# First attention of a two-layer block: last query rotation among the taps, ten taps moved, modulation products one tile later, row copy ahead of the exponentials

## The chip, the cores and the metric

The kernel runs on one core of one Trainium2 chip. The metric is the device time of one execution in microseconds (us). TensorE, VectorE, ScalarE and GpSimd are called PE, DVE, ACT and POOL, as the profile calls them. SP only issues transfers.

## The reference

Two transformer layers run on 1024 tokens of width 1024, all in float32. The change lies in the first layer. There the projection gives queries, keys and values of 8 heads of 64 and the two halves of a gated convolution. Queries and keys are rotated by position. Each token (a 16 x 64 grid) attends to a window of 8 x 16 neighbours and to 256 context tokens. Beside it a depthwise convolution of 31 taps runs over the gated half.

```python
def rope_half(xh, pos):                      # x1*cos - x2*sin, x2*cos + x1*sin
...
s_win = einsum(q_rot, k_window) * scale + bias      # 8 x 16 neighbours, biased by offset
s_ctx = einsum(q, k_ctx) * scale                    # 256 context keys, not rotated
p = softmax(concatenate([s_win, s_ctx]))
out = p_win @ v_window + p_ctx @ v_ctx
conv_x = silu(layer_norm(depthwise_conv(a * sigmoid(b), 31 taps) + bias))
x_new = x + g1 * (concatenate([attn, conv_x]) @ w_out)      # g1, sh2, sc2, g2: columns of silu(c) @ w_ada
```

The last line's g1 and the second norm's scale and shift are the "modulation": a product of one vector with a 1024 x 6144 matrix, of which 4096 columns (32 rows of 128) are computed during the attention, since they are not needed sooner.

## The kernel before, in words

Each engine runs its own instruction list in order, and the lists meet by semaphores. `sem(...)` names a counter, `reach(e, name, n)` makes engine e wait for it, and `free[0]` and `free[1]` count when the two halves of the accumulator `region` may be written again. `ch(...)` issues a DVE instruction and waits for it before the next one.

The projections come in units of 128 output columns. The last ones are u (gated half), k, v and q, four query units of two heads each. After a query unit ACT copies it twice (L748, L750). DVE rotates the second copy in `proj1_dve`: a shuffle (L797), two products (L798, L799) and two adds (L801). POOL splits the weights of later units into a high and a low part (L3006, L3009).

The attention (`na_*`) has 32 tiles. A tile is two heads and 128 queries (8 x 16 of the grid) against 640 keys. Tile i passes the engines so:

- PE, `scores(i)`: one row of the late modulation (`late_pe`, L630, into spare columns of `region` half 0), the turn of the row before (`late_turn_pe`, L636), then the scores (L971 context, L975 window).
- DVE, `most(i, s)` for the two heads s: adds the bias, writes `na_prob` and keeps the extreme (L1089). ACT, `exps(i, s)`: exponential with its sum (L1048). `late_act(i)` copies the modulation row out (L296, `late_row`). In before it runs between the two exponentials and gives `region` half 0 free.
- `norm(i)` one tile later: DVE takes the reciprocal (L1098) and scales one head (L1101), ACT the other (L1054). PE, `turn(i)`, transposes by matmul (L987, L992) in its own round i + 2. ACT moves four blocks of each head back to SBUF (`move`, L296, `na_prob_t`), DVE the fifth of both (L1107).
- PE, `values(i)`, in round i + 3: probabilities times values (L1008). ACT and DVE store the result as a high and a low part (`hi`, L296 `mixa_hi`; `lo`, L1113).

Beside this DVE works off the 124 convolution taps (`conv_tap`, L1164, 128x1024, in place on `conv`): 80 in the projection, 44 in the attention, one or two per tile. POOL adds finished groups of `conv` (`conv_sum_pool`, L1174). These three sums wait for all rotations and for 62, 93 and 124 taps.

SP's queue holds, in order, the loads of biases (384 KB, four buffers), of values (`v_pair`, 4 transfers of 64 KB a call) and of modulation weights (512 KB, two buffers, `late_load`). A late load waits until the row two before it is multiplied.

Of the kernel before, what the change touches and what calls it, by code (L numbers as in the profile page):

```python
# [25 lines left out]
ALU = mybir.AluOpType  # L26
ACT = mybir.ActivationFunctionType
# [3 lines left out]
T = 1024  # L31
# [4 lines left out]
CTX = 256  # L36
# [5 lines left out]
HD = 64  # L42
# [63 lines left out]
def build(nc, x_t, ctx_t, mem_t, w_ada, w_ada_late, units, small, rope_c, rope_s, na_bias, positions, out, x_spill,  # L106
# [58 lines left out]
    cos1 = place("cos1", [T], 160)  # L165
    late_row = place("late_row", [P], 178)
    v_ctx_raw = fixed("v_ctx_raw", [2, CTX], 28 * KIB)

# [469 lines left out]
    def late_act(e, n):  # L638
        reach(e, "late_used", 4 * (n + 1))
        copy(e, late_row[:], late_out).then_inc(sem("late_row"), 1)  # L640
        reach(e, "late_row", n + 1)
        e.sem_inc(free[0], 1)

# [61 lines left out]
    def proj1_act(e, pos, ch):  # L705
# [34 lines left out]
        for j in range(4):  # L740
            use = pos.next_use()
            e.wait_ge(unit_done, UNIT0["q"] + j + 1)
            if j < 2:
                reach(e, "v_tr", 3 + j)
            else:
                reach(e, "rope_done", 3 + j)
# [3 lines left out]
            e.activation(tmp[:, 2 + j % 2], region[:, use % 2], ACT.Copy, scale=HD ** -0.5).then_inc(free[use % 2], 1)  # L750
            if j == 0:
                v_out_act(3)

    def proj1_dve(e, pos, ch):
# [31 lines left out]
        for j in range(4):  # L786
# [3 lines left out]
            some_taps(6)  # L790
        for j in range(4):
            if j == 1:
                v_ctx_dve(e, 3)
            use = pos.next_use()
            e.wait_ge(free[use % 2], use // 2 + 1)
# [4 lines left out]
            for rb in range(2):  # L800
# [3 lines left out]
                else:  # L804
                    ch(last)
            reach(e, "rope_done", 5 + j)
        return taps

# [144 lines left out]
    def na_pe(e, pos):  # L953
        assert pos.use % 2 == 0

        def scores(i):
            j, q = divmod(i, TT)
# [6 lines left out]
            rows = [slice(0, 64), slice(64, 128)]  # L964
            for s in range(2):
                wait_region(e, uses[s])
            late_pe(e, i)
            if i:
                late_turn_pe(e, i - 1)
            for s in range(2):  # L970
# [44 lines left out]
        for i in range(NA_N + 3):  # L1015
# [4 lines left out]
            if i == NA_N:  # L1020
                wait_region(e, pos.use + 1)
                late_turn_pe(e, N_LATE - 1).then_inc(sem("late_tr"), 1)
            if i == NA_N + 1:
                wait_region(e, pos.use)
                ln_mean_pe(e)
# [4 lines left out]
    def na_act(e, pos, ch):  # L1030
# [25 lines left out]
        for i in range(NA_N + 4):  # L1056
            if i >= 4:
                hi(i - 4)
            if 1 <= i < NA_N + 1:
                norm(i - 1)  # L1060
            for s in range(2):
                if i < NA_N:
                    exps(i, s)
                if s == 0 and i < NA_N:
                    late_act(e, i)
                if 2 <= i < NA_N + 2:
                    move(i - 2, s)
# [8 lines left out]
    def bias_of(i):  # L1076
        j, q = divmod(i, TT)
        return 6 * j + 3 * (q // 4) + [0, 1, 1, 2][q % 4]

    def na_dve(e, pos, ch, taps):  # L1080
        def most(i, s):
# [5 lines left out]
            if s == 0:  # L1087
                reach(e, f"bias_ld{n % 4}", 16 * (n // 4 + 1))
            e.tensor_tensor_reduce(na_prob[:, i % 3, s], region[:, s, 0:KEYS], bias_t[n % 4][:, s], -1.0, 3.0e38,  # L1089
                                   ALU.add, ALU.min, na_neg[:, c:c + 1]).then_inc(sem("na_most"), 1)  # L1090
            if s:
                reach(e, "na_most", 2 * i + s + 1)
                e.sem_inc(free[s], 1)

# [15 lines left out]
        def lo(i):  # L1110
# [3 lines left out]
                            na_out(mixa_hi, j, q).bitcast(F32), ALU.subtract).then_inc(sem("na_lo"), 1)  # L1114

        left = list(taps)
        for n in range(1, 4):
            e.memset(bias_t[n][:, :, 0:CTX], 0.0).then_inc(sem("bias_zero"), 1)
        for i in range(NA_N + 4):
# [7 lines left out]
            if 2 <= i < NA_N + 2:  # L1127
                move(i - 2)
            for n in left[len(left) * i // NA_N:len(left) * (i + 1) // NA_N]:
                conv_tap(e, ch, n)  # L1130
            if i == NA_N:
                late_end_dve(e, ch)
                e.sem_inc(free[1], 1)
            if i > NA_N:
# [1778 lines left out]
    with nc.Block() as block:  # L2913
        @block.sync
        def _(sp):
# [30 lines left out]
            for cs in range(4):  # L2946
                v_pair_load(sp, 0, cs)
            late_load(0)
            late_load(1)
            reach(sp, "bias_zero", 4)  # L2950
            for n in range(1, 4):
                bias_load(sp, n)
            loads = iter(range(4, N_BIAS))
            for i in range(NA_N):
                if i + 2 < N_LATE:
                    late_load(i + 2)
# [405 lines left out]
```

## Time and profile before

| | us |
|---|---|
| median of three runs | 2526.86 (2525.43 to 2527.62) |
| the profiled execution's own time | 2529.12 |
| its span in the profile | 2527.3 |
| PE busy | 2407.3 (95%) |
| DVE, POOL, ACT busy | 1345.9, 968.6, 936.5 |
| mean granted clock of PE | 0.986 |

PE is busy for 95% of the span, but not evenly. The attention lies at 307 to 499 us, between the last query unit and the first output unit. There PE's share is lower (230 matmul records and 17.4 us busy in the 20 us from 420 to 440), and that stretch alone is changed.

### The profile page before, as it was taken

What the parts mean: (1) busy time and instruction counts of PE and PEld (TensorE: products, weight loads), DVE (VectorE), ACT (ScalarE), POOL (GpSimd) and SP (SyncE); (2) the same over time, 40 slices, a digit from 0 to 9 for tenths busy, and PEclk for the clock granted to TensorE, in tenths of its full rate; (3) what the DMA queues carried; (4) which work ended last, traced back from release to release, by engine and by line L of the source; (5) the groups of instructions that cost most, each with busy time, mean ns of one, the idle gap of its engine ahead of it and who ended that gap; (6) DMA issues with size and microseconds to landing.
All of it is one profiled execution on the core that took longest, in us unless ns stands there. A gap on an engine that the chain in (4) does not pass through costs nothing.

```text
span 2527.3 us, 34014 instructions
## 1 busy us (share of the span) xinstructions
PE 2407.3 (95%) x13374; PEld 1965.2 (78%) x13374; DVE 1345.9 (53%) x1566; ACT 936.5 (37%) x1541; POOL 968.6 (38%) x574
## 2 busy tenths in 40 slices
PE   6999888899999999999999899998999999999999
PEld 3788767677878888888877578877888888888877
DVE  3799678767732223222584977854410246454342
ACT  4301267625343234422554477752410111323220
POOL 1444300032255444544433310026134444787643
PEclk9999989999999999999999899999999999999999
DMA  6111266321121111111122300002011111111132
GB/s 268 42 42 57 83 186 184 114 88 45 43 63 51 42 55 62 56 34 55 54 109 67 143 25 2 1 26 84 18 50 50 42 50 51 66 52 43 50 125 92
DMA packets 66080, 175.12 MB, mean 69 GB/s; under 512 B 6724, under 2 KB 25416, under 8 KB 64392
## 3 DMA queue, kind: packets, MB, share of 16 engines
q1 hardware_dynamic: 59936, 149.66, 18.1%
q10 hardware_dynamic: 5992, 23.34, 2.4%
q8 instruction: 107, 1.75, 0.3%
q14 instruction: 45, 0.37, 0.0%
HBM read 161.89 MB, written 11.08 MB: 68 GB/s over the span
## 4 chain that ended last, share of the span: by engine, by line
PE 83%; DVE 10%; ACT 3%; issue 2%; DMA 1%; POOL 1%; SPq 0%; ACTq 0%; DVEq 0%; POOLq 0%
PE region L300 15%; PE region L302 15%; PE region L301 15%; PE region L2545 3%; PE region L2547 3%; PE region L2546 3%; PE aux L2545 3%; PE aux L2547 3%; PE aux L2546 3%; PE pv L2109 2%; PE aux L2099 2%; PE pv L300 2%; PE pv L301 2%; PE pv L302 2%; DVE conv L1164 1%
## 5 line engine op out<-in xcount | busy, mean ns | idle before, releaser
L3006 POOL TENSOR_TENSOR w_hi<-w_raw,der 128x1024 fp32r<-128x1024 f32 x96 | 192.3, 2003 | 889.8 <-PE region L302 834.8
L300 PE MATMUL region<-h_hi,w_hi 128*128 128x512 f32 x928 | 367.2, 396 | 10.6 <-issue 5.0
L301 PE MATMUL region<-h_lo,w_hi 128*128 128x512 f32 x928 | 364.4, 393 | 0.0
L302 PE MATMUL region<-h_hi,w_lo 128*128 128x512 f32 x928 | 363.7, 392 | 0.0
L2582 POOL TENSOR_TENSOR w_lo<-w_raw,w_hi 128x512 fp32r<-128x512 f32 x153 | 199.4, 1311 | 241.6 <-ACT w_hi L296 239.7
L3009 POOL TENSOR_TENSOR w_lo<-w_raw,w_hi 128x1024 fp32r<-128x1024 f32 x96 | 261.2, 2721 | 7.5
L300 PEld LDWEIGHTS region<-h_hi,w_hi 128*128 128x128 f32 x928 | 176.0, 190 | 54.9 <-issue 8.8
L302 PEld LDWEIGHTS region<-h_hi,w_lo 128*128 128x128 f32 x928 | 176.1, 190 | 37.3
L301 PEld LDWEIGHTS region<-h_lo,w_hi 128*128 128x128 f32 x928 | 176.1, 190 | 35.7
L296 ACT ACTIVATE w_hi<-w_raw 128x512 fp32r<-128x512 f32 (+1 forms) x159 | 100.2, 642 | 256.9 <-PE pv L302 85.1
L1164 DVE SCALAR_TENSOR_TENSOR conv<-glu,par,conv 128x1024 f32<-128x1024 f32 x120 | 188.2, 1568 | 3.4
L2582 POOL TENSOR_TENSOR w_lo<-w_slot,w_hi 128x512 fp32r<-128x512 f32 x57 | 75.3, 1327 | 107.6 <-ACT w_hi L296 107.1
L1438 DVE TENSOR_TENSOR ff_lo<-mlp_blk,ff_hi 128x512 fp32r<-128x512 f32 x56 | 50.1, 894 | 93.4 <-ACT ff_hi L296 93.3
L296 ACT ACTIVATE prob_t<-aux 128x512 f32<-128x512 f32 (+1 forms) x160 | 81.9, 554 | 47.6 <-PE aux L2099 37.3
L1609 DVE SCALAR_TENSOR_TENSOR x<-pv,der,x 128x1024 f32<-128x1024 f32 x28 | 35.9, 1283 | 117.8 <-PE pv L302 117.8
L2170 DVE TENSOR_REDUCE der<-region 128x1 f32<-128x1024 f32 x64 | 78.2, 1223 | 23.1 <-PE region L302 21.5
L300 PE MATMUL pv<-ff_hi,w_hi 128*128 128x512 f32 x224 | 87.8, 392 | 1.5 <-POOL w_lo L2582 0.8
L301 PE MATMUL pv<-ff_lo,w_hi 128*128 128x512 f32 x224 | 87.2, 389 | 0.0
L302 PE MATMUL pv<-ff_hi,w_lo 128*128 128x512 f32 x224 | 87.2, 389 | 0.0
L2545 PE MATMUL region<-h_hi,w_hi 128*128 128x512 f32 x204 | 79.4, 389 | 0.0
L2546 PE MATMUL region<-h_lo,w_hi 128*128 128x512 f32 x204 | 79.4, 389 | 0.0
L2547 PE MATMUL region<-h_hi,w_lo 128*128 128x512 f32 x204 | 79.4, 389 | 0.0
(481 smaller groups left out, 5884.8 us busy)
## 6 DMA issues: line engine op xcount, KB each, us to landing
w_raw<-units SPq DMA_DIRECT2D x122, 512.0 KB, 3.5
w_raw<-units SPq DMA_DIRECT2D x77, 256.0 KB, 2.6
w_raw<-w_ada_late SPq DMA_DIRECT2D x32, 512.0 KB, 4.3
bias<-na_bias SPq DMA_DIRECT2D x24, 384.0 KB, 4.0
w_slot<-units SPq DMA_DIRECT2D x35, 256.0 KB, 2.6
ada_buf<-w_ada SPq DMA_DIRECT2D x4, 2048.0 KB, 28.8
head_wide<-v_spill SPq DMA_DIRECT2D x16, 512.0 KB, 3.7
x_sb<-x_t ACTq DMA_DIRECT2D x2, 2048.0 KB, 14.1
```

The source lines that it names most:

```text
L296: return e.activation(dst, src, ACT.Copy, **kw)
L300: pe.matmul(dst, wh, xh, start=first, stop=False)
L301: pe.matmul(dst, wh, xl, start=False, stop=False)
L302: return pe.matmul(dst, wl, xh, start=False, stop=last)
L1164: ch(e.scalar_tensor_tensor(out=conv[:, j], in0=src, scalar=w, in1=conv[:, j], op0=ALU.mult, op1=ALU.add))
L2170: e.tensor_reduce(neg_max[:, m % 4:m % 4 + 1], region[:, s], AX, ALU.max, negate=True).then_inc(sem("mla_maxed"), 1)
L2545: e.matmul(dst, wh[:, w], xh[:, k], start=(j < 3 and k == 0), stop=False, skip_group_check=True)
L2546: e.matmul(dst, wh[:, w], xl[:, k], start=False, stop=False, skip_group_check=True)
L2547: last = e.matmul(dst, wl[:, w], xh[:, k], start=False, stop=(k == 3), skip_group_check=True)
L2582: e.tensor_tensor(w_lo[chunk_of(c)], chunks[c].src, w_hi[chunk_of(c)].bitcast(F32), ALU.subtract).then_inc(chunk_ready, 1)
L3006: pool.tensor_tensor(w_hi[:, s], w_raw[:, s], one_col.broadcast_to([P, 1024]), ALU.mult)\
L3009: pool.tensor_tensor(w_lo[:, s], w_raw[:, s], w_hi[:, s].bitcast(F32), ALU.subtract)\
```

## The change

Five things move, and no arithmetic is dropped.

1. The rotation of the fourth query unit leaves `proj1_dve`. It gets two buffers of its own (`q3_raw`, `q3_swapped`) and runs as four steps in DVE's rounds 2 to 5 of the attention. The unit is needed from tile 24 on.
2. Ten of the 44 taps left go into the query units (1, 3, 3 and 3), together with the three memsets of the bias buffers. 34 taps and the four rotation steps are spread over rounds 0 to 30, so none is left in round 31.
3. PE multiplies modulation row i - 1 in round i, behind the turn of row i - 2. The scores no longer wait for ACT's row copy but for DVE's `most` alone (`na_most`).
4. ACT copies row i - 1 after `most(i, 0)` and ahead of `exps(i, 0)`, and `hi` goes ahead of the second `move` instead of behind it.
5. SP's queue: bias 1 goes ahead of late load 1, the second pair's values move to rounds 5 to 8 behind the last rotation, and each round's late load goes last.

```diff
@@ late_act
         copy(e, late_row[:], late_out).then_inc(sem("late_row"), 1)
-        reach(e, "late_row", n + 1)
-        e.sem_inc(free[0], 1)
@@ proj1_dve
-        for j in range(4):
+        some_taps(1)
+        for j in range(3):
             if j == 1:
                 v_ctx_dve(e, 3)
+                some_taps(3)
+            if j == 2:
+                some_taps(3)
...
+        for n in range(1, 4):
+            e.memset(bias_t[n][:, :, 0:CTX], 0.0).then_inc(sem("bias_zero"), 1)
+        some_taps(3)
@@ na_pe
+        def late(n):
+            if n:
+                late_turn_pe(e, n - 1)
+            late_pe(e, n)
...
-            for s in range(2):
-                wait_region(e, uses[s])
-            late_pe(e, i)
             if i:
-                late_turn_pe(e, i - 1)
+                reach(e, "na_most", 2 * i)
+                late(i - 1)
+            else:
+                for s in range(2):
+                    wait_region(e, uses[s])
@@ na_act
-            if i >= 4:
-                hi(i - 4)
             if 1 <= i < NA_N + 1:
                 norm(i - 1)
             for s in range(2):
+                if s == 0 and 1 <= i < NA_N + 1:
+                    reach(e, "na_most", min(2 * i + 1, 2 * NA_N))
+                    late_act(e, i - 1)
                 if i < NA_N:
                     exps(i, s)
-                if s == 0 and i < NA_N:
-                    late_act(e, i)
+                if s == 1 and 3 <= i < NA_N + 3:
+                    hi(i - 3)
                 if 2 <= i < NA_N + 2:
                     move(i - 2, s)
@@ na_dve
-            if s:
-                reach(e, "na_most", 2 * i + s + 1)
-                e.sem_inc(free[s], 1)
...
+        def last_rope(step):
+            if step == 0:
+                e.wait_ge(free[last_use % 2], last_use // 2 + 1)
+                ch(e.stream_shuffle(q3_swapped[:], q3_raw[:], SWAP))
+            if step == 1:
+                ch(e.tensor_tensor(q3_swapped[:], q3_swapped[:], sin1[:], ALU.mult))
...
+            if 2 <= i < 6:
+                last_rope(i - 2)
+            for _ in range(0 if i >= LAST_TAP else share * (i + 1) // LAST_TAP - share * i // LAST_TAP - (2 <= i < 6)):
+                conv_tap(e, ch, left.pop(0))
@@ sync queue
+            reach(sp, "bias_zero", 4)
+            bias_load(sp, 1)
             late_load(1)
...
-                if i < 4:
-                    v_pair_load(sp, 1, i)
+                if 5 <= i < 9:
+                    if i == 5:
+                        reach(sp, "rope_done", 8)
+                    v_pair_load(sp, 1, i - 5)
...
+                if i + 2 < N_LATE:
+                    late_load(i + 2)
```

With `share = 38` and `LAST_TAP = 31` two slots fall to rounds 4, 8, 13, 17, 22, 26 and 30, seven of them; before there were twelve rounds with two taps.

The entry of the attention on DVE, before: the rotation of unit 3 (`q_rot_77`), the memsets, and the first tile's two `most` (ISA with `na_prob`).

```order
L797 STREAM_SHUFFLE tmp<-tmp 128x1024
L798 TENSOR_TENSOR tmp<-tmp,sin_78 128x1024
L799 TENSOR_TENSOR tmp<-tmp,cos_81 128x1024
L801 TENSOR_TENSOR q_rot_77<-tmp 128x8x4x16 x2
L1118 MEMSET bias_89 128x2x256
L1118 MEMSET bias_90 128x2x256
L1118 MEMSET bias_91 128x2x256
L1089 ISA na_prob,der<-region,bias_88 128x640
```

The same place now, from the rotation of unit 2 (`q_rot_76`) on:

```order
L1197 SCALAR_TENSOR_TENSOR conv<-glu,par,conv 128x1024 x3
L802 STREAM_SHUFFLE tmp<-tmp 128x1024
L803 TENSOR_TENSOR tmp<-tmp,sin_78 128x1024
L804 TENSOR_TENSOR tmp<-tmp,cos_81 128x1024
L806 TENSOR_TENSOR q_rot_76<-tmp 128x8x4x16 x2
L813 MEMSET bias_91 128x2x256
L813 MEMSET bias_92 128x2x256
L813 MEMSET bias_93 128x2x256
L1197 SCALAR_TENSOR_TENSOR conv<-glu,par,conv 128x1024 x3
L1106 ISA na_prob,der<-region,bias_90 128x640
```

The fourth rotation is gone from ahead of the first `most`, and three taps stand there in its stead; three more stand ahead of unit 2's rotation.

One tile on ACT in the middle of the attention, before: exponential, modulation row, move, exponential, move, high part of the output, scaling.

```order
L1048 ACTIVATE na_prob,der<-na_prob,der 128x640
L296 ACTIVATE late_row<-region 128x128
L296 ACTIVATE na_prob_t<-aux 128x512
L1048 ACTIVATE na_prob,der<-na_prob,der 128x640
L296 ACTIVATE na_prob_t<-aux 128x512
L296 ACTIVATE mixa_hi<-pv 128x8x16
L1054 ACTIVATE na_prob<-na_prob,der 128x640
```

And now:

```order
L298 ACTIVATE late_row<-region 128x128
L1062 ACTIVATE na_prob,der<-na_prob,der 128x640
L298 ACTIVATE na_prob_t<-aux 128x512
L1062 ACTIVATE na_prob,der<-na_prob,der 128x640
L298 ACTIVATE mixa_hi<-pv 128x8x16
L298 ACTIVATE na_prob_t<-aux 128x512
L1068 ACTIVATE na_prob<-na_prob,der 128x640
```

The row copy stands first, and the high part changes places with the second move.

## Rows read from the trace of the kernel before

**Rows 1.** Waits, 310 to 500 us: who waited, for whom, us total, times, longest.

```profile
ACT na_prob L1048 <- DVE der L1089: 30.3, 32, 7.3
...
PE region L630 <- DMA w_raw<-w_ada_late: 3.8, 1, 3.8
```

**Rows 2.** Timeline, one one-tap tile on DVE and ACT: start us, us, instruction.

```profile
360.89 0.82 DVE L1089 CUSTOM_DVE_ANT_0 na_prob<-region,bias 128x640 f32<-128x640 f32 x1
...
362.58 0.26 ACT L296 ACTIVATE late_row<-region 128x128 f32<-128x128 f32 x1
...
363.01 0.60 ACT L296 ACTIVATE na_prob_t<-aux 128x512 f32<-128x512 f32 x1 [0.17 <-ACT late_row L296]
...
363.50 0.82 ACT L1048 ACTIVATE na_prob<-na_prob,der 128x640 f32<-128x640 f32 x1
...
364.31 0.59 ACT L296 ACTIVATE na_prob_t<-aux 128x512 f32<-128x512 f32 x1
364.79 0.28 ACT L296 ACTIVATE mixa_hi<-pv 128x128 fp32r<-128x128 f32 x1
365.17 0.29 DVE L1113 TENSOR_TENSOR mixa_lo<-pv,mixa_hi 128x128 fp32r<-128x128 f32 x1 [0.88 <-ACT mixa_hi L296]
...
365.57 0.56 DVE L1101 TENSOR_SCALAR na_prob<-na_prob,der 128x640 f32<-128x640 f32 x1
366.04 0.82 DVE L1089 CUSTOM_DVE_ANT_0 na_prob<-region,bias 128x640 f32<-128x640 f32 x1
```

**Rows 3.** Timeline of DVE, one tile with two taps.

```profile
398.42 0.82 DVE L1089 CUSTOM_DVE_ANT_0 na_prob<-region,bias 128x640 f32<-128x640 f32 x1
...
400.55 2.60 DVE L1164 SCALAR_TENSOR_TENSOR conv<-glu,par,conv 128x1024 f32<-128x1024 f32 x2
...
404.05 0.82 DVE L1089 CUSTOM_DVE_ANT_0 na_prob<-region,bias 128x640 f32<-128x640 f32 x1
```

**Rows 4.** Timeline of PE, one round: first piece, window scores, last piece.

```profile
406.08 0.64 PE L630 MATMUL region<-w_raw,silu_wide 128*32 128x128 f32 x16 [0.74 <-ACTq L642]
...
407.51 0.82 PE L975 MATMUL region<-k_rot,q_rot 64*128 64x256 f32 x8
...
409.99 0.82 PE L1008 MATMUL pv<-na_prob_t,v_pair 128*64 128x128 f32 x12
```

**Rows 5.** Timeline: entry (memsets, tile 0, PE's round 1), tile 3, tile 31.

```profile
313.25 1.57 DVE L1118 MEMSET bias<- 128x512 f32 x3 [0.17 <-DVE q_rot L801]
...
314.73 0.76 DVE L1089 CUSTOM_DVE_ANT_0 na_prob<-region,bias 128x640 f32<-128x640 f32 x1
...
316.71 1.08 PE L630 MATMUL region<-w_raw,silu_wide 128*32 128x128 f32 x16 [7.63 <-ACTq L642]
...
334.27 0.82 DVE L1089 CUSTOM_DVE_ANT_0 na_prob<-region,bias 128x640 f32<-128x640 f32 x1
...
484.14 0.82 DVE L1089 CUSTOM_DVE_ANT_0 na_prob<-region,bias 128x640 f32<-128x640 f32 x1
```

**Rows 6.** Timeline: taps beside a weight split; rotation of unit 2; POOL's split.

```profile
241.05 10.10 DVE L1164 SCALAR_TENSOR_TENSOR conv<-glu,par,conv 128x1024 f32<-128x1024 f32 x5
...
300.91 1.42 DVE L801 TENSOR_TENSOR q_rot<-tmp 128x512 f32<-128x512 f32 x2
...
306.92 2.37 POOL L3009 TENSOR_TENSOR w_lo<-w_raw,w_hi 128x1024 fp32r<-128x1024 f32 x1
```

**Rows 7.** Windows, 316 to 324 us: length, busy PE, PEld, DVE, ACT, POOL, PEclk, DMA share, GB/s.

```profile
316.00:324.00 8.00, 4.03 (x30) 2.95 (x30) 5.24 (x11) 4.37 (x11) 0.00 (x0) 0.50 0.96 290
```

**Rows 8.** Timeline: DVE's scaling beside POOL's sums of `conv`.

```profile
369.58 2.37 POOL L1174 TENSOR_TENSOR conv_sum<-conv_sum,conv 128x1024 f32<-128x1024 f32 x1 [54.08 <-DVEq L1166]
...
370.65 1.65 DVE L1101 TENSOR_SCALAR na_prob<-na_prob,der 128x640 f32<-128x640 f32 x1
...
489.41 2.30 DVE L1101 TENSOR_SCALAR na_prob<-na_prob,der 128x640 f32<-128x640 f32 x1
```

**Rows 9.** The weight buffer's transfers, 295 to 500 us.

```profile
DMA to landing us min/median/max: 3.4/4.3/8.3
```

More of the change, by code:

```diff
@@ L166, in build @@
     late_row = place("late_row", [P], 178)
+    q3_raw = place("q3_raw", [T], 108)
+    q3_swapped = place("q3_swapped", [T], 124)
     v_ctx_raw = fixed("v_ctx_raw", [2, CTX], 28 * KIB)
@@ L744, in proj1_act @@
                 reach(e, "v_tr", 3 + j)
-            else:
-                reach(e, "rope_done", 3 + j)
+            elif j == 2:
+                reach(e, "rope_done", 5)
             for rb in range(2):
@@ L749, in proj1_act @@
                     .then_inc(sem("q_t"), 1)
-            e.activation(tmp[:, 2 + j % 2], region[:, use % 2], ACT.Copy, scale=HD ** -0.5).then_inc(free[use % 2], 1)
+            e.activation(q3_raw[:] if j == 3 else tmp[:, 2 + j % 2], region[:, use % 2], ACT.Copy, scale=HD ** -0.5)\
+                .then_inc(free[use % 2], 1)
             if j == 0:
@@ L1020, in na_pe @@
             if i == NA_N:
-                wait_region(e, pos.use + 1)
+                reach(e, "na_most", 2 * NA_N)
+                late(N_LATE - 1)
+            if i == NA_N + 1:
                 late_turn_pe(e, N_LATE - 1).then_inc(sem("late_tr"), 1)
-            if i == NA_N + 1:
-                wait_region(e, pos.use)
                 ln_mean_pe(e)
@@ L1078, in bias_of @@
         return 6 * j + 3 * (q // 4) + [0, 1, 1, 2][q % 4]
+    LAST_TAP = NA_N - 1
     def na_dve(e, pos, ch, taps):
@@ L1114, in lo @@
                             na_out(mixa_hi, j, q).bitcast(F32), ALU.subtract).then_inc(sem("na_lo"), 1)
+        last_use = pos.next_use()
+        def last_rope(step):
[4 more added lines that the diff above has]
+                ch(e.tensor_tensor(q3_swapped[:], q3_swapped[:], sin1[:], ALU.mult))
+            if step == 2:
+                ch(e.tensor_tensor(q3_raw[:], q3_raw[:], cos1[:], ALU.mult))
+            if step == 3:
+                ch(e.tensor_tensor(by_tile(q_rot[3], 0), by_row(q3_raw, 0), by_row(q3_swapped, 0), ALU.add))
+                e.tensor_tensor(by_tile(q_rot[3], 1), by_row(q3_raw, 1), by_row(q3_swapped, 1), ALU.add)\
+                    .then_inc(sem("rope_done"), 1)
         left = list(taps)
-        for n in range(1, 4):
-            e.memset(bias_t[n][:, :, 0:CTX], 0.0).then_inc(sem("bias_zero"), 1)
+        share = len(left) + 4
         for i in range(NA_N + 4):
@@ L1128, in na_dve @@
                 move(i - 2)
-            for n in left[len(left) * i // NA_N:len(left) * (i + 1) // NA_N]:
-                conv_tap(e, ch, n)
+            if 2 <= i < 6:
+                last_rope(i - 2)
+            for _ in range(0 if i >= LAST_TAP else share * (i + 1) // LAST_TAP - share * i // LAST_TAP - (2 <= i < 6)):
+                conv_tap(e, ch, left.pop(0))
             if i == NA_N:
+                reach(e, "na_most", 2 * NA_N)
+                e.sem_inc(free[0], NA_N)
+            if i == NA_N + 1:
                 late_end_dve(e, ch)
-                e.sem_inc(free[1], 1)
+                e.sem_inc(free[1], NA_N + 1)
             if i > NA_N:
@@ L2948, in _ @@
             late_load(0)
+            reach(sp, "bias_zero", 4)
+            bias_load(sp, 1)
             late_load(1)
-            reach(sp, "bias_zero", 4)
-            for n in range(1, 4):
-                bias_load(sp, n)
+            bias_load(sp, 2)
+            bias_load(sp, 3)
             loads = iter(range(4, N_BIAS))
             for i in range(NA_N):
-                if i + 2 < N_LATE:
-                    late_load(i + 2)
                 if i + 1 == NA_N or bias_of(i + 1) != bias_of(i):
```

## The prediction

> **What bounds the kernel now.** I read the page first: PE is busy 95% of the span, so only a stretch where PE idles has time to give. The change touches one such stretch, the first attention. There I read the waits, then one tile after another in the timeline. In the waits [rows 1] the reader is to see that ACT's exponentials wait 32 times for DVE's `most` (30.3 us), and that PE waits only once for a weight transfer (3.8 us). So the tiles are held by a ring between DVE and ACT, and PE follows it.
>
> The ring is read off one tile with one tap [rows 2]. From `most` (360.89) to `most` (366.04) it takes 5.15 us: `most` and first exponential 1.69, row copy 0.43 (0.17 of it a wait for its own result), first move 0.49, second exponential 0.81, second move 0.48, high part to DVE's low part 0.38, then low part and reciprocal 0.40 and scaling 0.47. A tile with two taps takes 5.63 [rows 3], since there DVE is never free. PE's round, first piece to last, is 406.08 to 410.81 or 4.73 us [rows 4], of which 2.25 us lead to the scores. PE has idled 0.74 us ahead of it. From tile 3 to tile 31 it is 149.9 us [rows 5], 5.35 a tile.
>
> The entry is slow too. PE is through with tile 0's scores at 309.1 (316.71 - 7.63), but DVE takes them at 314.73, behind the fourth rotation and the memsets. So PE stands still for 7.63 us and works on at a granted clock of 0.50, the lower level of 1.2 GHz [rows 5, 7]: 16 matmuls take 1.08 us there and 0.64 us in [rows 4]. Tile 3 starts at 334.27, three tiles after 19.5 us.
>
> **The change part by part.** Each sum is made inside the profiled execution (2529.12 us, span 2527.3) and then taken off the median of 2526.86, since that execution ran 2.3 us above it.
>
> *Steady tile.* On ACT the row copy leaves the middle of the ring and enters its front. Its own 0.26 us stays, the 0.17 us wait goes. The second move (0.48) leaves the ring, because the high part now goes ahead of it and DVE waits only for that. New ring: 1.69 + 0.26 + 0.49 + 0.81 + 0.38 + 0.40 + 0.47 = 4.50 us. The high part of tile i - 3 now needs the values of PE's same round. They end 4.73 us after the round's start; ACT comes to it at 2.25 + 0.86 + 0.26 + 0.83 + 0.49 + 0.81 = 5.5, so the wait is covered by 0.8 us. The second move feeds the second transposes of PE's next round; it ends about 1.7 us into that round and they stand some 2.7 us into it: covered by 1 us.
>
> *PE's start.* PE now waits for `most` of the second head, not for the row copy behind the exponential. From PE's start to the next start is 2.25 + 0.03 + two times 0.74 + 0.15 = 3.9 us, below PE's own round. PE's work is the same, its pieces reordered, with one more wait at the head. I take 4.65 (the range is 4.5, its weight loads alone, to 4.95, the 4.73 with two waits of 0.1 added). So the two rings lie within 0.2 us of each other, and I take 4.55 for a one-slot tile.
>
> *DVE.* The wait for its own `most` and the count behind it go: about 0.2 us. Two-tap tile 5.63 - 0.18 = 5.45, and 7 of them in place of 12. The four rotation steps have one tap's length each (1.2 to 1.4 us by their parts), so they cost what the taps they replace cost. Tiles 3 to 31: 21 x 4.55 + 7 x 5.45 = 133.7 us.
>
> *POOL against DVE.* A scaling that runs into POOL's sum of `conv` took 1.65 and 2.30 us in place of 0.55 [rows 8]; it ended 0.35 us after POOL. Before, one of the three sums fell on memsets, one on tile 9 (1.1 us) and one on the tail (1.75 us). Now all wait for the fourth rotation, at the end of DVE's round 5, when taps 62 and 93 are long done. Two sums follow each other there. The scaling of that round is due 0.7 us after the first sum starts and is held to its end: 1.5 us. If the second sum slips in first, 2.4 more; I leave that to the range. The third sum starts after the last tap of round 30 and holds that round's scaling: 1.8 us. So 133.7 + 3.3 = 137.0 us. In the tail that hold is gone, but the last modulation row is now multiplied there (0.6 on PE, 0.26 on ACT) and the high part waits for values: I take 0.4 us more, from -1 to 1.5.
>
> *Entry.* Without the fourth rotation DVE is done with unit 2's rotation at 302.3 at the earliest [rows 6], with the memsets (1.57 [rows 5]) at 304.0 and with three taps of 1.28 at 307.8 (two take 2.60 [rows 3]). PE's first scores then set tile 0 at 308.5. That is one end. But taps beside POOL's weight split are slower: five took 10.10 us, 3.7 over their 6.4 [rows 6]. Two of the three groups of taps now stand where the split of the next unit falls. The 3 ahead of unit 2's rotation delay it by some 1.5 us, and the last 3 meet the split that ends at 309.29 [rows 6]: 307.8 + 1.5 + 3.7 = 313.0. I take 313.0, since DVE and POOL are both busy there in every unit. The rotation products met the split before as well, so part of the cost was there already; hence the lower end of 308.5 stays.
>
> The Trainium skill (SBUF — State Buffer, the reading of its diagram of SBUF's ports) says that a DVE operation with two SBUF inputs and a POOL operation that reads SBUF lock each other out for a whole instruction. It speaks against putting taps into the query units; by it alone the entry would be the 313 of the sum, and without it 308.5.
>
> From 313.0 the first round follows. PE starts round 1 at 314.6, after 5.5 us without work. In the trace such a stop (7.63 us) ended at the lower clock [rows 5, 7]; I take it that the clock falls again. At the lower clock the 2.25 us to the scores become 3.8, by 1.08 against 0.64. Tiles 1 and 2 come at 318.2 (no row is turned yet) and 323.7, and PE is then busy without a break as it was before the clock came back in the trace, so tile 3 comes at 328. Before it was 334.27: 6.3 us gained. One stall of that 19.5 us was the late weight transfer, 3.8 us [rows 1]. It goes because tile 2's row is multiplied a round later and the 4 x 4 value loads have left its way.
>
> The Trainium skill (TensorE: Matmul & The Clock Gate, Part 1: The HAM clock gate) says that the monitor behind the clock runs freely, not from the kernel's start. By that an idle of 5.5 us may or may not be caught. The case not caught stands among the rivals.
>
> *SP's queue.* Late loads now stand behind the bias and value loads. From the issue of load i + 2 to its use there are two tiles less 0.8 us, 8.3 us; landing takes 3.4 to 8.3 us with 4.3 the median [rows 9]. Covered, barely so in the rounds with four value transfers (2 us of issue).
>
> *Sum.* Tile 31 before at 484.14. Now 328 + 137.0 = 465.0. The gain is 19.1, less 0.4 in the tail: 18.7. What follows the attention is unchanged. 2526.9 - 18.7 = 2508.2, rounded to 2508.5.
>
> **The rivals.**
>
> *PE becomes the bound.* Its round has 60 matmul records and four waits for other engines. If it runs at 4.95, 28 tiles take 138.6, the two-tap tiles hide in it and most of the 3.3 us of holds do not: some 141, so 4 us less gain, 2512.5. For it: 4.73 against 4.50 [rows 2, 4]. Against it: the 4.73 was measured with the waits inside the round already in it.
>
> The Trainium skill (TensorE: Matmul & The Clock Gate, Back-to-back issue gap) gives 81 ns for a sustained matmul of 128 columns. The 46 narrow ones would take 3.7 us by it, the round 5.3 and the kernel about 2520. The trace has the same 46 in 3.1 us, so I go by the row.
>
> *The entry comes out free.* The clock is not caught, or taps and splits do not meet: tile 3 at 321 to 325. The time is 2501.5 to 2505.5. For it: the idle shrinks from 7.6 to at most 5.5 us.
>
> *The gain does not come in the tiles.* A wait I did not see takes the place of the one removed, the high part on values for instance, and tiles stay at 5.1. Then 28 x 5.1 + 3.3 = 146 and the gain is 6.3 + 3.8 - 0.4, about 2517 to 2525. Against it: 0.8 us of cover.
>
> *Slower: the late weights land late.* Place: the twelve rounds with value loads and their neighbours. PE's round would stand on the transfer, as it did once [rows 1]. It decides once landing exceeds 8.3 us, the worst one in [rows 9], and each us more costs one us a round or half of one if it spreads. At 11.5 us in 12 rounds with two tiles behind each it takes back 19 us and more: 2530 to 2535. For it: DMA share 0.96 at the entry [rows 7] and shorter tiles. Against it: the same bursts before cost one wait in 32.
>
> **How the numbers follow.** Forecast (2505.5 to 2511) 0.45, PE as the bound (2511 to 2515) 0.2, entry free (2500 to 2505.5) 0.18, gain mostly lost (2515 to 2527) 0.11, slower 0.06. The range of 8 in 10 takes in the first three cases with their ends: 2501 to 2517. A change of 0.2% (5 us) is about what a measurement can tell from none. Faster by more than that 0.91, within it 0.04, slower 0.05.
>
> **What would show it right or wrong.** Tile 0's `most` near 313 us; PE's clock low for a stretch after it; `most` to `most` of 4.5 to 4.7 us in one-tap tiles and 5.45 in the seven others; the scaling of DVE's rounds 6 and 31 above 1.5 us; PE's idle ahead of a round near nothing, and no wait for `w_raw`. It is wrong if tiles stay above 5.0 us, if PE waits for `w_ada_late`, or if DVE's low part waits for a high part that waits for PE.

## The result, and the profile after

The changed kernel takes 2508.99 us (median of four runs, 2507.85 to 2510.61). The kernel before took 2527.24 us beside it (2525.43 to 2528.41). The ratio is 0.9925, with a 95% interval of 0.9913 to 0.9937: 18.3 us faster. The prediction was 2508.5. The profiled execution of after took 2510.61 us, its span is 2508.8 us and the mean granted clock 0.982.

Two executions reach the attention at moments that differ by up to 2.4 us, so stages are compared from PE's first piece of the attention to PE's first product of `mixa_hi`, the output projection. PE's timeline of before and of after has these rows (start, length, instruction):

```profile
307.15 0.65 PE L630 MATMUL region<-w_raw,silu_wide 128*32 128x128 f32 x16 [2.29 <-ACT tmp L750]
...
498.96 0.47 PE L300 MATMUL region<-mixa_hi,w_hi 128*128 128x512 f32 x1 [0.79 <-DVE mixa_lo L1113]
```

And after:

```profile
306.29 0.70 PE L985 MATMUL region<-k_ctx,q_t 64*128 64x256 f32 x4 [2.18 <-ACT q_raw L750]
...
479.13 0.47 PE L302 MATMUL region<-mixa_hi,w_hi 128*128 128x512 f32 x1 [0.82 <-DVE mixa_lo L1127]
```

The first `most` of tiles 0, 3 and 31 on DVE's timeline of after, to be read with [rows 5]:

```profile
311.96 0.82 DVE L1106 CUSTOM_DVE_ANT_0 na_prob<-region,bias 128x640 f32<-128x640 f32 x1
...
327.52 0.82 DVE L1106 CUSTOM_DVE_ANT_0 na_prob<-region,bias 128x640 f32<-128x640 f32 x1
...
461.93 0.81 DVE L1106 CUSTOM_DVE_ANT_0 na_prob<-region,bias 128x640 f32<-128x640 f32 x1
```

| us from span start | before | after | predicted for after |
|---|---|---|---|
| PE's first piece of the attention | 307.15 | 306.29 | |
| tile 0, first `most` | 314.73 | 311.96 | 313.0 |
| tile 3 | 334.27 | 327.52 | 328 |
| tile 31 | 484.14 | 461.93 | 465.0 |
| tiles 3 to 31 | 149.87 | 134.41 | 137.0 |
| first output product | 498.96 | 479.13 | |
| tile 31 to it | 14.8 | 17.2 | 15.2 |
| first piece to it | 191.8 | 172.8 | |

The stage is 19.0 us shorter, which is the gain to within a microsecond. Beside it the stage began 0.86 us earlier, and what follows the first output product took 1.4 us longer (2029.7 against 2028.3 us). In the twelve profiled executions of this document that remainder, whose work no kernel changes, took 2026.0 to 2031.4 us. The 95% intervals of the ratios are some 3 us wide to either side as well. So a difference of 2 or 3 us between two medians tells little by itself.

The waits of after, 310 to 500 us, answer to [rows 1]. The columns are the same.

```profile
ACT late_row L298 <- DVE der L1106: 24.5, 31, 2.7
DVE mixa_lo L1127 <- ACT mixa_hi L298: 14.9, 25, 3.5
...
PE region L632 <- DVE der L1106: 5.9, 1, 5.9
```

ACT's wait for `most` now stands at the row copy, the first thing that ACT does in a tile. PE's longest wait is its stop at the entry. It waits neither for ACT's row copy nor for a weight transfer. A one-tap tile, to be read with [rows 2], DVE and ACT in the order of their starts:

```profile
399.32 0.82 DVE L1106 CUSTOM_DVE_ANT_0 na_prob<-region,bias 128x640 f32<-128x640 f32 x1
...
400.18 0.28 ACT L298 ACTIVATE late_row<-region 128x128 f32<-128x128 f32 x1 [0.50 <-DVE der L1106]
400.35 0.82 ACT L1062 ACTIVATE na_prob<-na_prob,der 128x640 f32<-128x640 f32 x1
...
401.17 0.59 ACT L298 ACTIVATE na_prob_t<-aux 128x512 f32<-128x512 f32 x1
401.64 0.82 ACT L1062 ACTIVATE na_prob<-na_prob,der 128x640 f32<-128x640 f32 x1
...
402.45 0.27 ACT L298 ACTIVATE mixa_hi<-pv 128x128 fp32r<-128x128 f32 x1
402.61 0.60 ACT L298 ACTIVATE na_prob_t<-aux 128x512 f32<-128x512 f32 x1
402.83 0.29 DVE L1127 TENSOR_TENSOR mixa_lo<-pv,mixa_hi 128x128 fp32r<-128x128 f32 x1 [0.41 <-ACT mixa_hi L298]
...
403.23 0.55 DVE L1115 TENSOR_SCALAR na_prob<-na_prob,der 128x640 f32<-128x640 f32 x1
403.70 0.82 DVE L1106 CUSTOM_DVE_ANT_0 na_prob<-region,bias 128x640 f32<-128x640 f32 x1
```

From `most` to `most` it is 4.38 us. The steps are 0.86 to the row copy, 0.17 to the exponential, 0.82, 0.47, 0.81 to the high part, 0.38 to the low part, 0.40 to the scaling, 0.47. The second move starts after the high part, outside this ring. A tile with two taps, which answers to [rows 3], takes 5.32 us:

```profile
417.29 0.82 DVE L1106 CUSTOM_DVE_ANT_0 na_prob<-region,bias 128x640 f32<-128x640 f32 x1 [0.19 <-PE region L989]
...
419.12 2.60 DVE L1197 SCALAR_TENSOR_TENSOR conv<-glu,par,conv 128x1024 f32<-128x1024 f32 x2
...
422.61 0.82 DVE L1106 CUSTOM_DVE_ANT_0 na_prob<-region,bias 128x640 f32<-128x640 f32 x1
```

Its first row shows the second ring: DVE waited 0.19 us for PE's scores. PE's round, to be read with [rows 4], here from turn to turn of the modulation row:

```profile
329.64 0.38 PE L638 MATMUL region<-der,late_row 128*128 128x2 f32 x2
329.95 0.64 PE L632 MATMUL region<-w_raw,silu_wide 128*32 128x128 f32 x16
...
334.30 0.38 PE L638 MATMUL region<-der,late_row 128*128 128x2 f32 x2
```

That is 4.66 us without a gap. Tiles 7 to 30 take 107.03 us, 4.65 each, the same number. So here PE sets the mean. The one-tap tiles run faster than PE (4.38) until they meet it (4.56, 4.66), and fall behind in the two-tap tiles. By DVE's ring alone the mean of these 23 tiles, five of them with two taps, would be 4.58. The entry and its windows answer to [rows 5 to 7], with DVE, POOL and PE in the order of their starts:

```profile
303.17 1.57 DVE L813 MEMSET bias<- 128x512 f32 x3 [0.17 <-DVE q_rot L806]
...
304.19 3.38 POOL L3042 TENSOR_TENSOR w_hi<-w_raw,der 128x1024 fp32r<-128x1024 f32 x1 [4.98 <-PE region L304]
304.65 7.27 DVE L1197 SCALAR_TENSOR_TENSOR conv<-glu,par,conv 128x1024 f32<-128x1024 f32 x3
...
307.64 3.20 POOL L3045 TENSOR_TENSOR w_lo<-w_raw,w_hi 128x1024 fp32r<-128x1024 f32 x1
...
313.59 1.08 PE L632 MATMUL region<-w_raw,silu_wide 128*32 128x128 f32 x16 [5.95 <-DVE der L1106]
```

The windows have the columns of [rows 7]:

```profile
310.00:314.00 4.00, 0.41 (x8) 0.40 (x12) 3.97 (x6) 1.18 (x3) 0.84 (x1) 0.50 0.45 160
...
322.00:326.00 4.00, 4.00 (x36) 3.47 (x36) 2.42 (x7) 2.30 (x7) 0.00 (x0) 0.58 0.33 122
326.00:330.00 4.00, 4.00 (x48) 3.44 (x51) 3.93 (x9) 3.01 (x8) 0.00 (x0) 1.00 0.69 225
```

Three taps took 7.27 us beside POOL's split, against three times 1.28. PE stood still for 5.95 us and worked at 1.2 GHz (0.50) until about 325 us. POOL's sums against the scaling answer to [rows 8]:

```profile
340.70 2.36 POOL L1207 TENSOR_TENSOR conv_sum<-conv 128x1024 f32<-128x1024 f32 x1 [29.85 <-DVE q_rot L1142]
341.22 2.19 DVE L1115 TENSOR_SCALAR na_prob<-na_prob,der 128x640 f32<-128x640 f32 x1
...
459.29 2.37 POOL L1207 TENSOR_TENSOR conv_sum<-conv_sum,conv 128x1024 f32<-128x1024 f32 x1 [113.67 <-DVEq L1199]
459.70 2.31 DVE L1115 TENSOR_SCALAR na_prob<-na_prob,der 128x640 f32<-128x640 f32 x1
```

Both scalings end 0.35 us after POOL. The tiles with them take 5.94 and 7.20 us. The weight transfers answer to [rows 9]; the longest is shorter than before:

```profile
DMA to landing us min/median/max: 3.4/4.3/7.0
```

In the tail the clock fell. In the trace of before it stayed at 1.00 from 484 to 500 us. Windows of after, with the columns of [rows 7], and two rows of PE's timeline:

```profile
462.00:466.00 4.00, 0.67 (x5) 0.49 (x6) 2.43 (x9) 3.22 (x9) 0.00 (x0) 0.92 0.00 0
466.00:470.00 4.00, 4.00 (x38) 3.56 (x40) 0.74 (x2) 1.35 (x3) 0.00 (x0) 0.50 0.02 4
470.00:474.00 4.00, 4.00 (x25) 2.88 (x22) 0.98 (x4) 1.36 (x3) 0.00 (x0) 0.73 0.73 262
```

```profile
464.50 0.63 PE L1001 MATMUL aux<-ident,na_prob 128*128 128x128 f32 x4 [2.76 <-ACT na_prob_t L298]
465.96 1.09 PE L1001 MATMUL aux<-ident,na_prob 128*128 128x128 f32 x4 [0.83 <-ACT na_prob_t L298]
```

PE was nearly idle after the held scaling (0.67 us busy in 4), then worked 4 us at 1.2 GHz. This is the slowest of the four executions of after, with the lowest mean clock; the others had 0.985 to 0.987. Whether the clock fell in their tails is not known, since only this trace was kept.

### The profile page after: what moved, and what is told of

The parts are those of the page before. It is cut to its first block, busy times and chain, and to the rows that moved or that the text cites. A ratio compares the mean times of both kernels' runs of the same rounds, so it can differ in the third digit from the quotient of the medians.

```text
span 2508.8 us, 33978 instructions
## 1 busy us (share of the span) xinstructions
PE 2408.2 (96%) x13374; PEld 1967.6 (78%) x13374; DVE 1351.1 (54%) x1566; ACT 933.4 (37%) x1541; POOL 973.6 (39%) x574
## 3 DMA queue, kind: packets, MB, share of 16 engines
q1 hardware_dynamic: 59936, 149.66, 18.3%
## 4 chain that ended last, share of the span: by engine, by line
PE 85%; DVE 9%; ACT 2%; issue 2%; POOL 1%; DMA 1%; ACTq 0%; DVEq 0%; POOLq 0%
PE region L302 15%; PE region L304 14%; PE region L303 14%; PE region L2578 3%; PE region L2580 3%; PE region L2579 3%; PE aux L2578 3%; PE aux L2579 3%; PE aux L2580 3%; PE pv L2142 2%; PE aux L2132 2%; PE pv L302 2%; PE pv L304 2%; PE pv L303 2%; PE pv L1022 1%
## 5 line engine op out<-in xcount | busy, mean ns | idle before, releaser
L1197 DVE SCALAR_TENSOR_TENSOR conv<-glu,par,conv 128x1024 f32<-128x1024 f32 x120 | 194.7, 1623 | 3.2
```

What stands on the lines that cost most here:

```text
L1197: ch(e.scalar_tensor_tensor(out=conv[:, j], in0=src, scalar=w, in1=conv[:, j], op0=ALU.mult, op1=ALU.add))
```

## The experiments

Ten kernels, each compared with runs of the kernel before on its own chip (medians 2527.97, 2527.69 and 2527.51). "Stage" is the time from PE's first piece to the first output product, as above.

| kernel | median (range) | to before | ratio, 95% | stage | tile 0 | tiles 3 to 31 | tail |
|---|---|---|---|---|---|---|---|
| before | | | | 191.8 | 7.6 | 149.9 | 14.8 |
| after | 2508.99 | -18.3 | 0.9913 to 0.9937 | 172.8 | 5.7 | 134.4 | 17.2 |
| entry_only | 2537.4 (2533.0 to 2545.1) | +9.4 | 1.0027 to 1.0055 | 199.5 | 5.6 | 161.8 | 15.9 |
| entry_loads_first | 2526.92 (2523.8 to 2529.3) | -0.8 | 0.9992 to 1.001 | 187.0 | 5.6 | 150.3 | 14.9 |
| ring_only | 2507.26 (2507.1 to 2508.2) | -20.7 | 0.9907 to 0.9932 | 170.9 | 7.7 | 133.0 | 14.9 |
| hi_back | 2513.09 (2510.2 to 2517.8) | -14.9 | 0.9934 to 0.9959 | 180.0 | 5.7 | 142.4 | 16.3 |
| row_between | 2512.7 (2509.6 to 2516.6) | -15.0 | 0.9931 to 0.9958 | 174.9 | 5.7 | 136.8 | 16.4 |
| sums_timed | 2504.15 (2503.8 to 2504.8) | -23.8 | 0.9893 to 0.9921 | 167.4 | 5.7 | 131.3 | 14.9 |
| taps_back | 2506.1 (2504.9 to 2507.7) | -21.6 | 0.9903 to 0.993 | 170.4 | 1.4 | 137.0 | 17.2 |
| sums_taps | 2501.98 (2499.8 to 2502.9) | -25.7 | 0.9884 to 0.9914 | 166.8 | 1.4 | 134.2 | 16.4 |
| ring_sums | 2506.56 (2505.8 to 2508.2) | -21.0 | 0.9905 to 0.9933 | 170.8 | 7.7 | 132.9 | 14.9 |
| sums_taps_8 | 2501.64 (2499.1 to 2502.9) | -25.9 | 0.9883 to 0.9915 | 164.0 | 1.4 | 132.9 | 14.9 |

Tile 0 counts from PE's first piece, the tail from tile 31 to the first output product.

### The two halves of the change

entry_only is after with parts 3 and 4 undone: the order of PE's and ACT's rounds as before.

```diff
@@ late_act, scores and na_act of after
+        reach(e, "late_row", n + 1)
+        e.sem_inc(free[0], 1)
-                reach(e, "na_most", 2 * i)
-                late(i - 1)
+            late_pe(e, i)
+            if i:
+                late_turn_pe(e, i - 1)
```

> Parts 1, 2 and 5 alone: the fourth rotation and ten taps moved and SP's new order, but ACT, PE and DVE meet in a tile as before. My theory (entry and ring are two separate gains): tile 3 near 327, as in the changed kernel, since the entry is the same; one-tap tiles 5.15 us, two-tap tiles 5.6; 21 x 5.15 + 7 x 5.6 + 3.3 of holds = 150.7 from tile 3 to 31; about 7 us off the time before, 2520. Rival (the ring needs the entry's lower tap count, the entry gives little by itself): less than 3 us off, since the first tiles only run into the slower ring.

Measured: 9.4 us slower than before, where 7 us faster was expected. Its waits, 310 to 500 us, PE's and then SP's, where L1176 is the load of a bias:

```profile
PE region L632 <- DMA w_raw<-w_ada_late: 21.1, 10, 6.2
```

```profile
SPq L1176 <- DVE der L1101: 92.3, 20, 9.3
```

PE waited ten times for modulation weights. Their landing took 5.8 us at the longest, so they were issued late, not slow. SP's queue held the late load behind a bias load, and that waits for a tile's `most`. To test that, entry_loads_first moves one thing:

```diff
@@ sync queue of entry_only
             for i in range(NA_N):
+                if i + 2 < N_LATE:
+                    late_load(i + 2)
                 if i + 1 == NA_N or bias_of(i + 1) != bias_of(i):
...
-                if i + 2 < N_LATE:
-                    late_load(i + 2)
```

> Like the kernel with parts 1, 2 and 5 alone, which came out 9 us slower than before, but each round's late weight load goes ahead of the bias and value loads again. Theory (behind the bias load, which waits for most of the same round, the late load is issued one PE step too late for a row that is multiplied at the round's start): PE's 21 us of waits for w_raw vanish, tiles back at 5.15 and 5.6 us, about 151 us from tile 3 to 31, some 5 to 8 us faster than before, 2520 to 2523. Rival (the transfers are late because of the value loads moved to rounds 5 to 8 or the bandwidth): still slower than before.

Measured: as fast as before, 10.5 us faster than entry_only. The waits again:

```profile
PE region L632 <- DMA w_raw<-w_ada_late: 6.2, 1, 6.2
```

```profile
SPq L1176 <- DVE der L1101: 54.8, 20, 4.0
```

Nine of the ten waits are gone. The expected 2520 to 2523 did not come. The profiled execution, the fastest of eleven, has a stage 4.8 us shorter than before's and is 5.3 us shorter as a whole (2523.84 against 2529.12), but the median gives no gain. The other ten executions show a mean granted clock of 0.982 to 0.984, the profiled one 0.986, and those of before 0.984 to 0.989. So the clock may have taken the gain back; where, no kept trace shows. ring_only is the other half: before with parts 3 and 4 alone, its entry, taps and SP's queue untouched.

```diff
@@ scores and na_act of before
-            late_pe(e, i)
+                reach(e, "na_most", 2 * i)
+                late(i - 1)
...
+                if s == 0 and 1 <= i < NA_N + 1:
+                    late_act(e, i - 1)
                 if i < NA_N:
                     exps(i, s)
```

> Parts 3 and 4 alone: modulation products a round later, row copy ahead of the exponentials, high part ahead of the second move; the fourth rotation, all 44 taps and SP's order as before. Theory: tile 3 near 334 as before; one-tap tiles 4.37, two-tap tiles 5.32, now twelve of them; 16 x 4.37 + 12 x 5.32 = 133.8 and 1.1 for the one hold, 135 in place of 149.9 us; 15 us off the time before, 2512. Rival (PE's round of 4.66 us bounds, the tap count does not matter): the same within 1 us. Rival (the entry carries most of the gain): under 10 us off.

Measured: 20.7 us faster than before, where 15 was expected. The intervals of ring_only and of the whole change overlap, so parts 1, 2 and 5 brought nothing that these runs can tell. One sum of POOL holds a scaling inside its tiles (2.10 us), where after has two. Of its two-tap tiles ten lie between tile 3 and tile 31, where after has seven. DVE's timeline of ring_only, the first `most` of tiles 11 and 30:

```profile
366.93 0.82 DVE L1094 CUSTOM_DVE_ANT_0 na_prob<-region,bias 128x640 f32<-128x640 f32 x1
...
456.70 0.82 DVE L1094 CUSTOM_DVE_ANT_0 na_prob<-region,bias 128x640 f32<-128x640 f32 x1
```

These 19 tiles take 89.77 us, 4.72 each, and every one of them takes 4.37, 4.38 or 5.32. So here DVE's ring sets the mean, and PE waits after two-tap tiles. It lies only 0.07 us a tile above PE's round, so the three tiles more cost next to nothing: 133.0 less the hold of 1.5 us is 131.5, against 131.3 in sums_timed below, which has seven and no hold.

### The two orders on ACT

hi_back puts the high part behind the second move again.

```diff
@@ na_act of after
-                if s == 1 and 3 <= i < NA_N + 3:
-                    hi(i - 3)
                 if 2 <= i < NA_N + 2:
                     move(i - 2, s)
+                if s == 1 and 3 <= i < NA_N + 3:
+                    hi(i - 3)
```

> The changed kernel with the second move put back ahead of the high part, nothing else. Theory (the DVE-ACT ring sets a one-tap tile): 4.37 + 0.47 = 4.85 us per one-tap tile, two-tap tiles unchanged at 5.32, so a mean of 4.97 against 4.66: 28 x 0.31 = 8 to 9 us slower than the changed kernel, 2517 to 2518. Rival (PE's own round of 4.66 us bounds and has slack for it): 0 to 3 us slower.

Measured: one-tap tiles of 4.86 or 4.87, tiles 3 to 31 in 142.4 us, 8.0 more than after. Timeline of ACT and DVE in one tile of hi_back:

```profile
405.37 0.59 ACT L298 ACTIVATE na_prob_t<-aux 128x512 f32<-128x512 f32 x1
405.84 0.28 ACT L298 ACTIVATE mixa_hi<-pv 128x128 fp32r<-128x128 f32 x1
...
406.23 0.29 DVE L1127 TENSOR_TENSOR mixa_lo<-pv,mixa_hi 128x128 fp32r<-128x128 f32 x1 [0.90 <-ACT mixa_hi L298]
```

The move's 0.47 us stands in the ring again. The medians differ by less than the 8 to 9 us expected, 4.1 us against after, and the runs of hi_back scatter over 7.6 us. In its profiled execution what follows the attention took 2026.0 us, 3.7 less than in after; why is open.

row_between puts the row copy between the exponentials again and leaves the rest.

```diff
@@ na_act of after
+                if i < NA_N:
+                    exps(i, s)
                 if s == 0 and 1 <= i < NA_N + 1:
                     late_act(e, i - 1)
-                if i < NA_N:
-                    exps(i, s)
```

> The changed kernel with ACT's row copy put back between the two exponentials, still of the row before. Theory (the copy costs 0.17 us of the ring wherever it stands, and the gain there was the end of the wait and of PE's wait on it): within 1 us of the changed kernel, one-tap tiles 4.35 to 4.40. Rival (its place ahead of the exponentials is what matters, since the exponential's wait hides it): 0.1 to 0.2 us more per one-tap tile, 2 to 5 us slower.

Measured: 3.7 us slower than after by the medians, where less than 1 was expected. The runs of the two overlap, so the trace has to carry this: tiles 3 to 31 take 2.3 us more. Its waits, 310 to 500 us:

```profile
PE region L638 <- ACT late_row L298: 5.8, 8, 2.1
```

DVE's ring is hardly longer (4.42 or 4.43 us where it is alone, against 4.38). What grew is PE's round, which after a two-tap tile waits for the copy (5.09 or 5.10 us from its first piece to the next, against 4.66 to 4.83 in after).

### POOL's sums

sums_timed makes each sum wait until a scaling is through.

```diff
@@ conv_sum_pool of after
+    SUM_AFTER = [6, 7, 31]
         for j in range(1, 4):
             reach(e, "conv_done", j + 1)
+            reach(e, "na_prob", SUM_AFTER[j - 1])
```

> The changed kernel, but POOL's three sums of conv wait for the scalings of tiles 5, 6 and 30, so that each starts together with DVE's most of the next tile instead of beside a scaling. Theory (POOL and DVE lock each other out for a whole instruction): the two long scalings (2.19 and 2.31 us) fall to 0.55; tiles 5 to 6 and 30 to 31 take 4.4 and 5.3 us in place of 5.94 and 7.20; PE does not idle 3 us after tile 30, its clock stays up in the tail (it fell for 6.8 us there), tail 15 us in place of 17.2. 4 to 6 us less than the changed kernel, 2503 to 2505. Rival (the long scalings only fill time in which DVE would wait for PE anyway): under 1 us.

Measured: 2504.15 us, as expected. Timeline of DVE and POOL in sums_timed, the first sum:

```profile
341.11 0.55 DVE L1115 TENSOR_SCALAR na_prob<-na_prob,der 128x640 f32<-128x640 f32 x1
...
341.83 2.37 POOL L1210 TENSOR_TENSOR conv_sum<-conv 128x1024 f32<-128x1024 f32 x1 [31.09 <-DVE na_prob L1115]
```

The scaling takes 0.55 again, and the sum runs behind it. From tile 5 to 6 and from 30 to 31 it takes 4.30 and 5.43 us in place of 5.94 and 7.20. The sum itself does not get longer.

### The taps at the entry

taps_back gives the three taps behind the memsets back to the tiles, which makes ten two-slot tiles of seven.

```diff
@@ proj1_dve of after
             e.memset(bias_t[n][:, :, 0:CTX], 0.0).then_inc(sem("bias_zero"), 1)
-        some_taps(3)
```

> The changed kernel without the three taps between the memsets and tile 0; they go back into the attention, 37 taps over rounds 0 to 30, ten two-slot rounds instead of seven. Theory (these three took 7.3 us beside POOL's split and hold up tile 0; PE's round of 4.66 us is the mean bound in the tiles, and (21 x 4.37 + 10 x 5.32) / 31 = 4.68 stays at it): tile 0 4.2 us earlier, the clock not or later down, tile 3 6 to 8 us earlier, tiles the same within 1 us; 2501 to 2504. Rival (DVE's taps are the bound in the attention, 0.95 us each): 3 us of the gain lost, 2505 to 2507. Rival (the first late weights land no earlier and take the place of the wait): 0 to 3 us faster only.

Measured: 2506.1 us, where 2501 to 2504 was expected, with tile 0 4.3 us and tile 3 5.0 us earlier after the first piece than in after. Timeline of POOL and DVE in taps_back:

```profile
304.19 1.89 POOL L3041 TENSOR_TENSOR w_hi<-w_raw,der 128x1024 fp32r<-128x1024 f32 x1 [4.99 <-PE region L304]
...
307.65 0.82 DVE L1105 CUSTOM_DVE_ANT_0 na_prob<-region,bias 128x640 f32<-128x640 f32 x1 [2.91 <-PE region L988]
```

Without taps beside it POOL's split takes 1.89 us, not 3.38, and DVE waits for PE's scores. Tiles 3 to 31 take 2.6 us more. A third scaling is held (2.11 us), which is 1.6 of it. The rest is DVE's ring with ten two-slot tiles: from tile 9 to 30 it is 98.71 us, 4.70 each and above PE's 4.66. sums_taps is taps_back with the sums placed as in sums_timed.

> Both: the three taps back in the attention and POOL's sums starting with most of tiles 6, 7 and 31. Theory: both gains add, 4.5 + 7, 2496 to 2500. Rival (with the holds gone DVE has no more idle and PE's 4.66 us round swallows one of them): 2500 to 2504.

Measured: 2501.98 us, so the two gains do not add in full; the rival expected that. One held scaling was left, 2.11 us in round 8, as the group of 93 taps is finished only after the scaling that the second sum waited for. sums_taps_8 waits for rounds 6, 8 and 31.

> The whole change with the three taps behind the memsets given back to the attention and POOL's sums held until DVE's scalings of rounds 6, 8 and 31 are through (it was 6, 7 and 31). The one held scaling that was left (2.11 us, a tile of 5.90) should go: tiles 3 to 31 in 134.24 - 1.0 to 1.5 = 132.7 to 133.2 us, and the time 2500.5 to 2501 against 2501.98. Rival: PE's round of 4.66 is the mean bound, so DVE has slack after the held tile and takes the loss back in the next ones; then tiles 3 to 31 stay at 134 and the time at 2502.

Measured: no scaling above 0.6 us, tiles 3 to 31 in 132.9 us, 1.35 less. The median moved by 0.3 us, inside the scatter of both. These two are the fastest kernels here, 7.0 and 7.3 us faster than the whole change by the medians.

ring_sums holds back the second and the third sum of ring_only.

```diff
@@ conv_sum_pool of ring_only
+    SUM_AFTER = [0, 9, 32]
             reach(e, "conv_done", j + 1)
+            if j > 1:
+                reach(e, "na_prob", SUM_AFTER[j - 1])
```

> The kernel before with parts 3 and 4 alone, and POOL's second and third sum held until DVE's scalings of rounds 9 and 32 are through. If the rest of the change (rotation moved, ten taps into the query units, SP's order) is worth nothing once POOL's holds are out of both, this kernel equals the whole change with the sums placed, 2504.2 us, or lies up to 1.5 us above it, since its own tail has one hold less to lose: tiles 3 to 31 in 131.5 us against 133.0 of the ring alone, 2505 us. If the entry parts are worth the 2 to 4 us that their first tile and their missing DVE work suggest, it stays at 2507 or above, since PE's first stop of 7.9 us stays. Rival: the waits for DVE's scaling delay the last sum and with it the norm behind the attention, and it comes out slower than the ring alone, 2508 or more.

Measured: 2506.56 us. It missed its aim: I took the wrong round for the second sum, the scaling at 359.84 still takes 2.11 us, and tiles 3 to 31 stay at 132.9. So what parts 1, 2 and 5 are worth with well-placed sums has only a rough upper bound: 23.8 less 21.0, or 2.8 us, about 1.5 of which is this hold. The intervals of the two ratios overlap, so it may be nothing.

## Why the prediction was right, point by point

The time was right to 0.5 us, but two terms missed by 2 to 3 us each, in opposite directions: the tiles were shorter, the tail was longer. What follows the attention was called unchanged and took 1.4 us longer in these two executions, and 0.3 us of the agreement is rounding (the sum was 2508.2). Part of the agreement is luck.

- **The ring, 4.50 predicted: right in kind, 4.38 measured.** The row copy adds 0.17 us, not 0.26, since the exponential starts before the copy is through (400.18 to 400.35). hi_back shows the term of the second move by itself: 0.48 predicted, 4.86 - 4.38 = 0.48 measured.
- **Two-tap tile, 5.45: 5.32 measured.** Leaving out the wait for its own `most` was worth 0.31, not 0.18.
- **PE's round, 4.65: 4.66 measured, but its role was mis-told.** I added tile lengths as if each tile were its own race, with 4.55 as a mark-up for PE. In truth PE sets the mean in after, and DVE's fast and slow tiles average out around it. Without the two holds (1.64 and 1.77 us, by the tiles of after and of sums_timed) tiles 3 to 31 took 131.0 against the 133.7 predicted. The lower end of 4.5, "its weight loads alone", stands in no row: in the round of [rows 4] they are busy for 3.89 of 4.73 us. The rival "PE becomes the bound" was right in its mechanism and wrong in its price: the round did not grow to 4.95.
- **POOL's holds, 3.3 predicted: 3.4 measured**, at both places, and sums_timed takes 3.1 us of tiles and 4.8 us of median away with them.
- **Tail, 0.4 predicted: 2.4 measured.** This step failed. The tail was summed at full clock, and PE's idle of 2.76 and 0.83 us was followed by 0.50 in the windows. The four kernels with the same work in the tail whose clock stayed up (ring_only, ring_sums, sums_timed, sums_taps_8) all have 14.9, so what changed in the tail costs 0.1 us net and the other 2.3 are the clock's. The fall is not tied to the held scaling alone. In sums_taps nothing is held there, PE idles 1.08 and 0.83 us ahead of two turns, and the clock falls too (0.51 from 460 to 462 us, tail 16.4). In sums_taps_8 the same idle times leave it at 1.00 (tail 14.9). Here are PE's same sixteen matmuls in these two, first sums_taps, then sums_taps_8:

```profile
460.11 1.08 PE L632 MATMUL region<-w_raw,silu_wide 128*32 128x128 f32 x16
```

```profile
459.07 0.64 PE L632 MATMUL region<-w_raw,silu_wide 128*32 128x128 f32 x16
```

  With the same gaps one execution worked at 1.2 GHz and one at 2.4. The Trainium skill (TensorE: Matmul & The Clock Gate, Part 1: The HAM clock gate) says that the monitor runs freely; these two rows agree with that. I had allowed for that luck at the entry and not in the tail.
- **Entry, tile 0 at 313.0: 311.96, of which 0.86 is the earlier start.** From PE's first piece that is 5.67 us; the prediction, made in before's times, says 5.85. The taps met the split as summed: 7.27 us, against 3 x 1.28 + 3.7 = 7.5. taps_back shows the reason: they are what holds tile 0. The clock fell and came back, and tile 3 came 21.2 us after the first piece (20.9 predicted).
- **What brought the entry's 6.3 us was mis-told.** The sum gave it to the missing rotation and to the late load's stall. From the first piece to tile 3 before takes 27.1 us, the whole change 21.2, ring_only 23.0 and entry_only 21.9. So either half alone brings most of the 5.9 us, 4.1 or 5.3, and they do not add. ring_only keeps the rotation, the taps and SP's order of before, and its PE waits for no weight transfer, where before waited 3.8 us. The product one round later is enough to end that stall; the value loads did not have to move.
- **SP's queue, costed at nothing: right for the whole, for a reason that I had not seen.** The rival "late weights land late" put its point at a landing above 8.3 us. In entry_only the weights came late with landings of 5.8 at most. The cause was the wait of the bias load at the head of the queue. In the whole change it does no harm, since PE multiplies a row only after that same `most`: PE waits for no weight transfer in after. So the late load behind the bias load needs the later product of part 3. What part 5 brings beside part 3 no run shows.
- **"The gain does not come in the tiles" fell.** The high part waited for values three times, all in the tail (1.4, 3.5 and 1.4 us), and never in a steady tile.

## What to carry to other kernels

When two rings lie within a few per cent, compare their sums over many tiles, not their lengths in one tile: the engine with constant rounds sets the mean, and slow tiles of the other cost nothing until its mean is longer. Here PE led with seven two-tap tiles (4.65 us a tile) and DVE with ten (4.72). Before work is pulled ahead into a stage where another engine is busy on SBUF too, its price there is to be measured: three taps cost 7.3 us at the entry and 3.8 elsewhere. In a queue that issues its loads in order, as SP's does here, look at what each load's wait is waiting for, not only at how long the loads take to land.

## What the runs showed of the hardware that was not expected

- The stretching goes both ways. POOL's split took 3.38 and 3.20 us beside three taps and 1.89 and 2.34 without them, while the taps took 7.27 us in place of 3.84. Together that is 6.6 us for POOL where 4.2 would do, and DVE is through only after POOL.
- A scaling that starts during POOL's sum ended 0.34 to 0.36 us after it, in all nineteen pairs in the traces of this document, and took 1.65 to 2.31 us in place of 0.55. The sum kept its 2.35 to 2.37. In that pair only DVE pays. The tap that met the second sum of sums_timed took 1.85 us against 1.27 alone, less than a scaling loses.
- The clock fell in one execution (sums_taps) and not in another (sums_taps_8) on the same pattern of gaps, and that was worth 1.5 us in a tail of 15.
